# Stick-breaking attention by pairs of heads, with a step behind each half of a projection slot

## What is computed

```python
def stick_breaking_attention(q, k, v):          # per head, blocks of 128 queries
    strict = key_pos[None, :] < q_pos[:, None]
    z = jnp.einsum('bthd,bshd->bhts', qb, k).astype(jnp.float32) * (HEAD_DIM ** -0.5)
    brk = jnp.where(strict, jax.nn.softplus(z), 0.0)
    later = jnp.pad(brk[..., 1:], ((0, 0), (0, 0), (0, 0), (0, 1)))
    remain = lax.cumsum(later, axis=3, reverse=True)
    log_a = jax.nn.log_sigmoid(z) - remain
    a = jnp.where(strict, jnp.exp(log_a), 0.0).astype(v.dtype)
    o = jnp.einsum('bhts,bshd->bthd', a, v)

def odd_mixer(h, w_qkv, w_out):                 # h is the normed x
    q, k, v = jnp.split((h @ w_qkv).reshape(b, t, 3, C_HEADS, HEAD_DIM), 3, axis=2)
    return stick_breaking_attention(q[:, :, 0], k[:, :, 0], v[:, :, 0]) @ w_out
```

## Time and profile before

| | us |
|---|---|
| median of 3 runs | 1457.0 (1456.62 to 1458.64) |
| the profiled execution | 1458.65 |
| its span, first to last instruction | 1456.9 |
| TensorE busy in it | 1342.7 (92%) |
| GpSimd, VectorE, ScalarE busy | 1024.4, 763.1, 692.6 |
| mean granted TensorE clock | 0.951 of full speed |

### The profile page before, as it was taken

One profiled execution on the slowest core, in us unless ns is written; L12 is line 12 of the kernel. 1 busy time (PEld: TensorE's weight loads), 2 busy tenths in 40 slices (PEclk: granted clock), 3 DMA queues, 4 the chain that ended last, 5 costly groups with the idle time before them and its releaser, 6 DMA issues.

```text
span 1456.9 us, 28057 instructions
## 1 busy us (share of the span) xinstructions
PE 1342.7 (92%) x10930; PEld 1289.1 (88%) x10930; DVE 763.1 (52%) x1286; ACT 692.6 (48%) x965; POOL 1024.4 (70%) x797
## 2 busy tenths in 40 slices
PE   4788999999979779999998959999999999999999
PEld 4777999999979659999998847999999977899999
DVE  7996775555663777555566685511114146521112
ACT  7613554443655676434446445534435345544342
POOL 1033988888768707888877572888887960688885
PEclk9798999999989789999999878999999989999999
DMA  6401555555437403554553430455554540345540
GB/s 244 163 12 42 198 182 192 176 182 193 145 127 212 171 1 125 180 194 173 175 189 130 173 116 18 162 194 177 176 192 158 194 155 1 116 174 178 192 150 29
DMA packets 33877, 217.05 MB, mean 149 GB/s; under 512 B 3683, under 2 KB 7428, under 8 KB 8196
## 3 DMA queue, kind: packets, MB, share of 16 engines
q1 hardware_dynamic: 29808, 209.05, 40.6%
q10 hardware_dynamic: 3988, 6.85, 1.8%
HBM read 213.26 MB, written 2.62 MB: 148 GB/s over the span
## 4 chain that ended last, share of the span: by engine, by line
PE 73%; DVE 18%; issue 4%; ACT 3%; POOL 0%; DMA 0%; DVEq 0%; ACTq 0%; POOLq 0%
PE up L1290 18%; PE up L1291 17%; PE up L1292 17%; PE acc L1290 5%; PE acc L1292 5%; PE acc L1291 5%; DVE sq L746 2%; DVE x L1022 1%; DVE s_work L887 1%; DVE mix L1064 1%; PE acc L1713 1%; PE side L1442 1%; DVE mix L750 1%; DVE mix L1182 1%; DVE opnd L730 1%
## 5 line engine op out<-in xcount | busy, mean ns | idle before, releaser
L302 POOL TENSOR_TENSOR w_lo<-ring,w_hi 128x512 fp32r<-128x512 f32 x764 | 987.2, 1325 | 323.1 <-ACT w_hi L364 322.2
L1290 PE MATMUL up<-opnd,w_hi 128*128 128x256 f32 x2272 | 653.1, 287 | 21.1 <-DVE opnd L730 7.6
L1291 PE MATMUL up<-opnd,w_lo 128*128 128x256 f32 x2272 | 647.6, 285 | 0.0
L1292 PE MATMUL up<-opnd,w_hi 128*128 128x256 f32 x2272 | 647.3, 285 | 0.0
L364 ACT ACTIVATE w_hi<-ring 128x2048 fp32r<-128x2048 f32 x197 | 375.9, 1910 | 301.7 <-PE up L1292 241.8
L1290 PEld LDWEIGHTS up<-opnd,w_hi 128*128 128x128 f32 x2272 | 440.9, 194 | 28.1 <-issue 12.9
L1291 PEld LDWEIGHTS up<-opnd,w_lo 128*128 128x128 f32 x2272 | 441.0, 194 | 0.5
L1292 PEld LDWEIGHTS up<-opnd,w_hi 128*128 128x128 f32 x2272 | 440.9, 194 | 0.0
L1290 PE MATMUL acc<-opnd,w_hi 128*128 128x256 f32 x736 | 209.1, 284 | 5.2 <-DVE x L995 2.7
L1291 PE MATMUL acc<-opnd,w_lo 128*128 128x256 f32 x736 | 208.3, 283 | 0.0
L1292 PE MATMUL acc<-opnd,w_hi 128*128 128x256 f32 x736 | 208.2, 283 | 0.0
(11 more groups left out here) (241 smaller groups left out, 1403.4 us busy)
## 6 DMA issues: line engine op xcount, KB each, us to landing
ring<-in_stream SPq DMA_DIRECT2D x197, 1024.0 KB, 4.8
bias_rows<-mix ACTq DMA_DIRECT2D x1, 1536.0 KB
x<-in_x SPq DMA_DIRECT2D x1, 1024.0 KB, 5.8
mix<-in_s_b ACTq DMA_DIRECT2D x1, 1024.0 KB, 9.5
mix<-in_s_c ACTq DMA_DIRECT2D x1, 1024.0 KB, 14.1
mix<-bias_rows ACTq DMA_DIRECT2D x1, 1024.0 KB, 5.4
out_x<-x SPq DMA_DIRECT2D x8, 128.0 KB, 1.7
mix<-in_p ACTq DMA_DIRECT2D x2, 256.0 KB, 2.6
```

The source lines that it names most:

```text
L302: ins = nc.gpsimd.tensor_tensor(w_lo[:, b, cols], ring[:, r, cols], w_hi[:, b, cols].bitcast(f32), ALU.subtract)
L1290: MM(o, l_hi, r_hi, start=start, stop=False, skip_group_check=True)
L1291: MM(o, l_lo, r_hi, start=False, stop=False, skip_group_check=True)
L1292: return MM(o, l_hi, r_lo, start=False, stop=stop, skip_group_check=True)
```

## The change

The twelve projection slots are taken in the order `STICK_ORDER` and each is cut into two halves of 24 matmuls. There are 30 half steps t. Behind half step t TensorE does at most one step for a pair of heads: logits of pair p at `t = STICK_AT[p]`, sums two half steps later, values three later. VectorE, ScalarE and the copies follow at t+1 to t+4. All elementwise work of a pair is one instruction over 768 columns where there were two over 384, and `k_z` holds three pairs where it held six heads. The matmuls of a pair stand side by side, even head and odd head alternating. Half steps 24 to 29 have no projections left; the first two output slots are cut up to fill them (`fill`), and their last feature tiles both stand at t = 29. SyncE takes the stage's slots from a list and the rest in two loops. The core of the diff:

```diff
...
+STICK_ORDER = ["v0", "k0", "q0", "k1", "q1", "v1", "k2", "q2", "v2", "k3", "q3", "v3"]
+STICK_AT = [6, 8, 10, 12, 16, 18, 22, 23]
+STICK_HALVES = 30
...
+def stick_pair(t):
+    return STICK_AT.index(t) if t in STICK_AT else None
...
+def streamed(s):
+    i = s - START["qkv"]
+    if 0 <= i < len(STICK_ORDER):
+        kind, g = STICK_ORDER[i][0], int(STICK_ORDER[i][1])
+        return START["qkv"] + (g if kind == "v" else 4 + 2 * g + (kind == "q"))
+    return s
...
-            (KT, T), (KT, T), (TT, D), (384,), (P,), (6, 384), (2, 384), (2, 384), (2, 384), (2, T))
+            (KT, T), (KT, T), (TT, D), (384,), (P,), (3, 768), (2, 768), (2, 768), (2, 768), (2, T))
...
+            def listed(first, end):
+                for s in range(first, end):
+                    sp.wait_ge(sem("w_ready"), s - RING + 1)
+                    load(s % RING, slice(streamed(s), streamed(s) + 1))
...
-            for n in range(STICKS + 5):
...
+            for t in range(STICK_HALVES):
+                if t % 2 == 0:
+                    high_parts_to(S + min(t // 2, 12) + 2)
+                p = stick_pair(t - 3)
+                if p is not None:
+                    c.wait("log_a")
+                    if p >= 2:
+                        c.wait("stick_pv")
+                    c.up(A(k_a[:, p % 2], k_z[:, p % 3], ACT.Exp), "a_sb")
+                p = stick_pair(t - 1)
+                if p is not None:
                     c.wait("z_abs")
+                    b = k_t[:, p % 2]
+                    c.up_and_wait(A(b, b, ACT.Exp, scale=-1.0), "act_step")
+                    c.up(A(b, b, ACT.Ln, bias=1.0), "log1p")
+                p = stick_pair(t - 4)
+                if p is not None:
+                    act.wait_ge(sem("stick_pv"), p + 1)
+                    from_psum("stick", p, aux[p % 2][:, 0:T], k_out)
             residual("ffn3", START["out"])
             ffn(3, None)
...
             S, u0 = START["qkv"], BANK["qkv"]
             c.wait("rstd_tok")
...
-            for n in range(8):
...
+            def stick_projection(i):
+                kind, g, u = STICK_ORDER[i][0], int(STICK_ORDER[i][1]), (u0 + i) % 2
+                if kind == "v":
+                    values(S + i, u, k_v[:, :, g * 256:(g + 1) * 256], 256)
+                    c.tell("up_free")
+                else:
+                    dve.wait_ge(sem("mm_done"), S + i + 1)
+                    over_rms((k_k if kind == "k" else k_q)[:, 2 * g:2 * g + 2], u)
+                c.tell("stick_qkv")
...
-            for n in range(STICKS + 3):
...
+            mask = k_mask.unsqueeze(1).broadcast_to([P, 2, 384])
+            for t in range(STICK_HALVES):
+                if t % 2 == 0 and 2 <= t <= 24:
+                    stick_projection(t // 2 - 1)
+                p = stick_pair(t - 2)
+                if p is not None:
+                    c.wait("log1p")
+                    c.up(V.scalar_tensor_tensor(k_b[:, p % 2], k_z[:, p % 3], 0.0, k_t[:, p % 2], ALU.max, ALU.add),
+                         "brk")
+                p = stick_pair(t - 3)
+                if p is not None:
+                    c.wait("remain")
+                    z = heads(k_z[:, p % 3])
+                    c.up(V.tensor_tensor(z, z, acc[:, 2:4, 0:384], ALU.subtract), "log_a")
+                p = stick_pair(t - 1)
+                if p is not None:
                     c.wait("z_ps")
+                    if p >= 3:
                         c.wait("a_sb")
+                    c.up_and_wait(V.scalar_tensor_tensor(heads(k_z[:, p % 3]), acc[:, 0:2, 0:384], HD ** -0.5, mask,
+                                                         ALU.mult, ALU.add), "z_sb")
+                    if p >= 2:
+                        dve.wait_ge(sem("brk"), p - 1)
+                    c.up(V.scalar_tensor_tensor(k_t[:, p % 2], k_z[:, p % 3], -1.0, k_z[:, p % 3], ALU.mult, ALU.max),
                         "z_abs")
+                p = stick_pair(t - 4)
+                if p is not None:
+                    low_of("stick", p, k_out)
             residual("ffn3", START["out"], BANK["out"])
             ffn(3, None)
...
-            def slot_part(name, s, o, ks):
+            def slot_part(name, s, o, ks, fresh=True):
...
+                    if fresh:
+                        c.wait("hi_ready")
+                        c.wait("lo_ready")
...
-            token_slot("odd", S, fresh=True)
...
-            token_slot("odd", S + 1)
-            token_slot("odd", S + 2)
-            token_slot("odd", S + 3)
-            for n in range(8):
-                up_slot("odd", S + 4 + n)
...
-            for n in range(STICKS + 4):
...
-                    slot_part("stick", START["out"], first, [n // 2 - 4])
...
+            def stick_half(i, half, o):
+                b, token = (S + i) % SPLIT, STICK_ORDER[i][0] == "v"
+                for k in range(4 * half, 4 * half + 4):
...
+                if half:
+                    c.up(ins, "mm_done")
...
+            def stick_logits(p):
+                pe.wait_ge(sem("stick_qkv"), 1 + STICK_ORDER.index(f"q{p // 2}"))
+                if p:
+                    c.wait("z_sb")
+                for q in range(2):
+                    for e in range(2):
+                        r = slice(HD * e, HD * e + HD)
+                        ins = MM(acc[:, e, q * T:T + q * P], k_k[r, p, q * P:q * P + P], k_q[r, p, q * P:T],
+                                 start=True, stop=True, skip_group_check=True)
+                c.up(ins, "z_ps")
...
+            def stick_remain(p):
+                c.wait("brk")
+                if p:
+                    c.wait("log_a")
+                for e in range(2):
+                    o, b = acc[:, 2 + e], k_b[:, p % 2, 384 * e:384 * e + 384]
+                    MM(o[:, 0:T], k_tri, b[:, 0:T], start=True, stop=False, skip_group_check=True)
+                    MM(o[:, P:T], ones, b[:, T:T + P], start=False, stop=False, skip_group_check=True)
+                    ins = MM(o[:, T:T + P], k_tri, b[:, T:T + P], start=False, stop=True, skip_group_check=True)
+                c.up(ins, "remain")
...
+            def stick_values(p):
+                c.wait("a_sb")
+                pe.wait_ge(sem("stick_qkv"), 1 + STICK_ORDER.index(f"v{p // 2}"))
+                if p >= 2:
+                    pe.wait_ge(sem("hi_ready"), KT * UNIT["stick"] + p - 1)
+                for q in range(2):
+                    for e in range(2):
+                        h, r = 2 * p + e, HD * e
+                        ins = MM(aux[p % 2][r:r + HD, q * P:T], k_v[:, q, h * HD:(h + 1) * HD],
+                                 k_a[:, p % 2, 384 * e + q * T:384 * e + T + q * P], start=(q == 0), stop=(q == 1),
+                                 tile_position=(0, r), skip_group_check=True)
+                c.up(ins, "stick_pv")
...
+            out = START["out"]
+            fill = {24: [(0, range(4))], 25: [(0, range(4, 6)), (1, range(2))], 26: [(1, range(2, 6))],
+                    28: [(0, [6]), (1, [6])], 29: [(0, [7]), (1, [7])]}
+            banks = {}
+            for t in range(STICK_HALVES):
+                i, half = t // 2, t % 2
+                if i < 12:
+                    if half == 0:
+                        o = begin_slot(S + i)
+                    stick_half(i, half, o)
+                    if t == 1:
+                        rms(True)
+                for g, ks in fill.get(t, []):
+                    if ks[0] == 0:
+                        banks[g] = begin_slot(out + g)
+                    slot_part("stick", out + g, banks[g], ks, fresh=(g == 0))
+                if t == 5:
+                    pe.wait_ge(dma["stickmask"], 32)
+                p = stick_pair(t - 3)
+                if p is not None:
+                    stick_values(p)
+                p = stick_pair(t - 2)
+                if p is not None:
+                    stick_remain(p)
+                p = stick_pair(t)
+                if p is not None:
+                    stick_logits(p)
+            for g in range(2, 4):
+                up_slot("stick", out + g)
             ffn(3, "ffn3")
...
```

More of the change, by code:

```diff
@@ L248, in program, with heads @@
         (k_k, k_q, k_v, k_mask, k_tri, k_z, k_t, k_b, k_a, k_out) = carve(
-            (KT, T), (KT, T), (TT, D), (384,), (P,), (6, 384), (2, 384), (2, 384), (2, 384), (2, T))
+            (KT, T), (KT, T), (TT, D), (384,), (P,), (3, 768), (2, 768), (2, 768), (2, 768), (2, T))
+        def heads(v):
+            return v.rearrange("p (e q) -> p e q", e=2)
         def by_parity(v):
@@ L275, in _, with steady @@
             sp.wait_ge(sem("s5_cm"), 8)
-            turns = N_SLOTS // RING - 1
-            with sp.Fori(0, turns) as i:
-                for r in range(RING):
-                    sp.wait_ge(sem("w_ready"), i * RING + (r + 1))
-                    load(r, bass.ds(i * RING + (RING + r), 1))
-            for s in range(RING * (turns + 1), N_SLOTS):
-                sp.wait_ge(sem("w_ready"), s - RING + 1)
-                load(s % RING, slice(s, s + 1))
```

(62 more changed lines are left out.)

63 lines of the change are left out of this document (removed).

## The result

The changed kernel takes 1441.66 us (median of 4 runs, 1440.85 to 1442.53) against 1456.87 us (4 runs, 1456.62 to 1458.64) for the kernel before: a ratio of 0.9893, with a 95% interval of 0.9876 to 0.9910. That is 15.2 us less by the medians; the forecast was 13.1 less and 1443.9 us.

The account below looks back on a forecast made before the run. TensorE was taken as the bound, busy 92% of the span. Terms of 30.3 + 3.0 + 0.3 + 1.1 + 3.0 + 1.6 = 39.3 us replace 52.4, 13.1 less: 1443.9 us, range 1440 to 1450.

Parts of the forecast that it names:

- Pairs side by side: Logits and values on TensorE: two heads cost what one does; eight pairs, sums included, take 30.3 us.
- The sums: Sums on TensorE use the whole array and gain nothing from pairing: 2 x 1.07 us a pair.
- switching: Changes between projection passes and head steps on TensorE: returns 1.9 us, values or logits standing first 1.1, together 3.0.
- The start: First heads: the 9.4 us lost to waits and half clock go; lateness from logits to sums costs 0.3 for the stage.
- The end: End of the stage: pair 6's subtraction stands behind pair 7's softplus on VectorE, so TensorE waits 1.1 us.
- The clock: Granted TensorE clock: falls after the waits around slots 162 and 163, 1.6 us added.
- slots: Output slots in the tail: slots 160 and 161 end together, so TensorE waits 3.0 us before slots 162 and 163.
- Rival 1: VectorE against GpSimd: every late operation of a pair meets GpSimd, 5.8 us in place of 1.4: 1448.3; chance 0.15.
- Rival 2: Pairs do not overlap between projection passes or in alternating order; 13.1 us come back: 1457.0, no change; chance 0.08.
- Rival 3: Slower by the clock: small waits at the sums lower it inside the mixed stage, 17 us lost: 1461; chance 0.07.
- Rival 4: Better: no TensorE wait but the 3.0 us in the tail, and no clock fall: 1440.9; chance 0.10.

Follow-up runs that it names:

- e2: The changed kernel with the last feature tile of the half slot (six passes) between the two heads of a pair, for logits and values: 1457.16 us.
- e3: The kernel before, with only logits and values of two heads side by side on TensorE in every second turn: 1446.00 us, ratio 0.9922.
- e5: The changed kernel with VectorE's subtraction for a pair ahead of the softplus of the next: 1441.07 us.
- e6: The changed kernel with slot 163's high part made earlier and the bank told free before the first tile's low part, in the last residual: 1439.71 us.
- the control: The changed kernel itself, measured again for comparison on the same chip as follow-up runs: 1441.62 us, ratio 0.9890.
- e4: The changed kernel with pairs 0 to 3 at half steps 8, 10, 12, 14 and not 6, 8, 10, 12: 1439.64 us.
- e9: The changed kernel with pairs 0 to 5 at half steps 10, 12, 14, 16, 17, 18: 1440.69 us in its one run.
- e8: The changed kernel with GpSimd's low parts in eight pieces of 256 columns and not four of 512, everywhere: 1423.8 us in its one run.

## Why the prediction was right

*Pairs side by side.* Right in mechanism and size: 0.86 and 0.80 for two heads against 0.86 and 0.79 forecast, and e2 and e3 show that this carries most of the gain.

*The sums* were mis-sized. I took 2 x 1.07 = 2.14 for a pair from the earlier trace rows. A pair measures 1.84 when logits follow and 1.67 when passes follow (1169.80 to 1171.47). The 1.07 held about 0.2 us of changes from and to matmuls of another shape. Between the two heads of a pair there are none, and the one behind a pair was charged again under switching. The trace of before had it: the first step of the sums takes 0.53 us behind logits (from 1207.57 in the earlier trace rows) and 0.43 behind a pass (from 1211.10).

```profile
1208.10 0.38 PE L1714 MATMUL acc<-mix,par 128*128 128x128 f32 x2
...
1211.53 0.39 PE L1714 MATMUL acc<-mix,par 128*128 128x128 f32 x2
```

Work and switching were 33.3 in the sum; 37.0 less the 5.8 of waits leaves 31.2, 2.1 less.

*The start.* The 9.4 us went; the clock was 1.00 in the whole stage. What took their place was one step's error. I bounded an operation that meets GpSimd by one piece (at most 1.1 us), with the Trainium skill (SBUF — State Buffer, SBUF: two separate sides) behind it, which says that the loser blocks for the winner's whole instruction. The trace shows L1301 held through three pieces of 1.26 us, the first already begun, and with eighths through eight of 0.70; the measurement decides, and the bound does not hold in general. Elsewhere, in the other seven L1301 and in the second long run, it does. The earlier trace rows gave only the longest of each line. The trace of before has four held operations (1.28, 1.04, 1.62 and 1.04 us), all beside one run of four pieces from 1185.79 to 1191.68, and VectorE came in between its pieces each time; none of these four stood in a long run. The hold of pair 0 cost 1.9 us at the sums instead of 0.3.

*The end* was right: 1.29 against 1.1, for the reason given (e5), and 2.63 against 3.0 (e6).

*The clock* behind the waits was charged 1.6 us and did not come as extra. In the changed kernel the clock was 0.50 for 3.4 us from 1248.9, as in the control and as around the 3.1 of the earlier trace rows. It comes once, behind `ffn3`'s own wait of 1.88 us, and the waits of 0.91 and 1.72 ahead of it brought none. Which wait is followed by a fall is not settled: in e4 the same 3.4 us came behind the wait before slot 163 (1.73 us) and none behind `ffn3`'s, and e9, with all three waits, had no fall at all. The prediction also misread the fall at the start: it put it behind four waits, but the clock was already 0.50 from 1187.9 on the earlier trace rows, while the fourth wait ended at 1190.61.

So 13.1 was too small by 2.1 (sums) + 1.6 (clock) + 0.4 (slots), and too large by 1.6 (pair 0) + 0.2 (pair 6): 15.4, as measured. The errors partly cancelled.

*The rivals.* Rival 1 occurs in one pair of eight, and there one operation was held for 3.0 us, longer than the 2.2 it had put for two. The argument against it, that GpSimd would run beside softplus, did not hold: it ran beside the absolute value in all eight pairs. Rival 2 is what e2 built, at 1457.2 against the 1457.0 worked out for it. Rival 3 did not occur: the mixture of passes and head steps kept full clock even with waits of 1.9 and 1.3 us. In e8, at the wait of 4.18 us, the clock did fall inside the stage, for 3.4 us. Rival 4 gave 1440.9 from other terms.

## What to carry to other kernels

Before hiding small matmuls behind large ones, set those that use different halves of the array side by side: here two heads cost what one did in either order, and that alone gave about three quarters of the gain with three edited lines. Price an operation by the distance between starts in a back-to-back run, since durations overstated VectorE's load, and take the changes of shape out before adding them as a term of their own, since they were counted twice in the sums. Where GpSimd and VectorE both read SBUF, look at whether a critical VectorE operation falls into a long run of GpSimd; it can be held to the end of it, and need not be.

## What was not expected of the hardware

A VectorE operation with two SBUF inputs, 0.96 us where nothing holds it, took 4.00, 3.27 and 6.29 us and ended 0.81 to 0.82 us behind an unbroken run of GpSimd, while in another such run narrower ones came in at 1.52 us or less; operations of the same stage that read PSUM (L1297, L1291) kept 0.94 to 0.96 us throughout. Halving GpSimd's pieces made GpSimd's own work 18% longer per column and the kernel 15 us faster, with VectorE's work ahead of the stage 36 us shorter.
